# Decays of two chunks moved in the queues of a gated-delta projection

## The chip, the cores and the metric

The kernel runs on one core of a Trainium2 chip. The core has a matrix engine (TensorE, PE in the profile, with its weight loads as PEld), a vector engine (VectorE, DVE), an activation engine (ScalarE, ACT), a general engine (GpSimd, POOL) and a sync engine (SyncE, SP) that issues most DMAs. Each engine takes its instructions strictly in the order of its own queue, and waits on semaphores that other engines raise. The metric is the device time of one execution in microseconds (us), of which the median of several runs is taken.

## The reference

Two model blocks run one after the other on 512 tokens of width 1024, in float32: a block with differential and latent attention, memory cross attention and a mixture of experts, and then a block whose first layer is a gated delta rule mixer (six heads of width 128). The change lies in this mixer. Cut to what matters:

```
proj = h @ w_in                                  # 26 column tiles of 128 here
qkv  = silu(causal_depthwise_conv(proj[..., :o1], conv_w))
g    = -exp(a_log) * softplus(a_logit + dt_bias) # log decay per token and head
gc    = cumsum(chunks(g))
decay = exp(where(tril, gc[:, None] - gc[None, :], -inf))
lower = where(strict, (kb @ k.T) * decay, 0)
sol   = triangular_solve(lower, rhs, unit_diagonal=True)
intra = (q @ k.T) * decay
# a scan over the chunks then carries the state and gives the outputs
mem_o = memory_attention(mem_q, mem_k, mem_v)    # 4 heads, next to the mixer
```

The kernel uses four chunks of 128 tokens in place of the reference's shorter ones; the result of the recurrence is the same.

## The kernel before

The program is one long list of stages. Each stage adds instructions to the queues of the engines that it uses, so the order in which stages are listed is the order in every queue; nothing is reordered later. Ordering by hand is the whole schedule.

A projection is a `Linear`. Its weights come in column tiles. For each tile ScalarE rounds the raw weights to a high part (line 236), VectorE makes the low part (line 242), both two tiles ahead of use, and TensorE runs 24 matmuls (lines 299 to 301: eight input slices, three products each) into one of two PSUM banks. VectorE then takes the tile out of its bank (line 2536 in the mixer). A tile may start when its low weights are ready and when the bank of the tile two before it was taken out.

The mixer's projection is the `Linear` called gdnin, with 26 tiles numbered from 0. Tiles 0 and 1 are memory queries, 2 to 7 keys, 8 to 13 values, 14 to 19 queries, 20 to 25 gates. From tile 2 to 19 each tile is also convolved over time by VectorE (`convolve`, lines 2544 and 2546) and passed through SiLU by ScalarE (line 2526, one tile later). Other work of the mixer and of the memory attention is hung on the tiles by hand. `at_tile(j, ...)` puts stages behind tile j: on TensorE after its 24 matmuls, on ScalarE and VectorE after its weight split and its taking out, ahead of the convolution. `in_tile(j, ...)` puts them in the middle: on TensorE between the tile's two halves of 12 matmuls, on ScalarE and VectorE ahead of all of the tile's own work.

The stages that matter here:

- `decay(c, banks, free)` makes the decay matrices of chunk c for six heads, three in each of two banks, ps_out and ps_shared (q = 0 and 1). TensorE: 12 instructions in the trace (six products, line 2651). VectorE: six instructions that subtract the column sums and add a mask (line 2669). ScalarE: two exponentials of three heads (line 2696). TensorE waits for what `free` names, so that a bank isn't overwritten before it was read. Chunks 0 and 1 use the same two banks.
- The memory attention of four heads: `scored(n)` (scores on TensorE, line 892; maximum on VectorE, lines 1003 and 1004; exponentials on ScalarE, line 957), `weighed(n)` (division by the sum on VectorE, line 1032), `turned_over(n)` (transposes on TensorE, line 904; copies on ScalarE, line 973), `summed(n)` (values on TensorE, line 923).
- `key_norm(h)` and `query_norm(h)`: transposes (line 2714) and squared sums on ScalarE (line 2723), in the same two banks.
- `products(0)` behind tile 12, `turned_root(0)` behind tile 13 (copies, line 2823), and then the levels l = 1 to 5 of the triangular inverse of chunk 0, one a tile from tile 14 on: `step_u` in the tile (TensorE line 2659, ScalarE copies line 2840) and `step_r` behind it (TensorE line 2659, VectorE update line 2861). GpSimd masks a matrix for each level (line 2806).

Before the mixer's chunks GpSimd also rescales the residual in eight pairs of instructions (lines 2343 and 2344), beside the first tiles. ScalarE holds one table of functions at a time: SiLU and the exponential lie in different ones, and the trace shows a table load ahead of each switch.

Of the kernel before, what the change touches and what calls it, by code (L numbers as in the profile page):

```python
# [115 lines left out]
class Events:  # L116
# [24 lines left out]
    def need(self, eng, name, label):  # L141
        self.wait(eng, name, self.plan[name, label])
# [7 lines left out]
def program(nc, a, plan):  # L150

    with ExitStack() as ctx:
        ev = Events(nc, ctx, plan)
        done, need, step = ev.done, ev.need, ev.step
# [37 lines left out]
        ps_o, ps_m = (ctx.enter_context(nc.psum_tensor(n, [P, 512], F32)) for n in ("ps_out", "ps_shared"))  # L192
# [1430 lines left out]
        def cross_root_tile(act):  # L1623
# [5 lines left out]
                          vector=lambda dve: need(dve, "norm_act", ("cross", "R")))  # L1629
# [1015 lines left out]
        state_banks = (ps_o, ps_m)  # L2645
# [26 lines left out]
        def decay(c, banks, free):  # L2672

            def tensor(pe):
                need(pe, "gate_dve", "incl")
                for q in range(2):
                    need(pe, *free(q))
                    three(pe, banks[q], q, lambda h: col_of(GATE, c, h).to_broadcast([P, P]), lambda h: INCT, ("e", c, q))

            def vector(dve):  # L2680
                for q in range(2):
                    need(dve, "c_pe", ("e", c, q))
                    if c == 2:
                        need(dve, "conv_act", FIRST_Z - 1)
                    elif c == 3:
                        need(dve, "c_pe", ("tr", 0, q))
                    need(dve, "gate_dve", "gc")
                    three_scaled(dve, q, lambda h: DEC[c][:, h, :], lambda n, h: pair(banks[q])[:, n, :],
                                 lambda h: col_of(GC, c, h), lambda n, h: const("prev"), ALU.subtract, ALU.add,
                                 ("e", c, q))  # L2690

            def scalar(act):
                for q in range(2):
                    need(act, "c_dve", ("e", c, q))
                    h0, h1 = halves[q]
                    done(act.activation(DEC[c][:, h0:h1, :], DEC[c][:, h0:h1, :], ACT.Exp), "c_act", ("e", c, q))
            return On(tensor=tensor, vector=vector, scalar=scalar)
# [5 lines left out]
        def key_norm(h, bank, free):  # L2703
            return square_norm("k", h, lambda c: kT(h, c), FIRST_K + h, SSK, bank, free)

        def query_norm(h, bank, free):
            return square_norm("q", h, lambda c: qT(h, c), FIRST_Q + h, EQ, bank, free)
# [100 lines left out]
        def turned_root(c):  # L2808
            banks = chain_banks[c]

            def tensor(pe):
                for q in range(2):
                    need(pe, "c_dve", ("R", c, 0, q))
                    last = three_blocks(pe, banks[q], q, 0, RC[c], None)
                    done(last, "c_pe", ("T", c, q))

            def scalar(act):
                for q in range(2):
                    h0, h1 = halves[q]
                    need(act, "c_pe", ("T", c, q))  # L2820
                    if c == 0:
                        need(act, *att_mem0.last)
                    done(act.copy(TC[c][:, h0:h1, :], pair_c(banks[q], 0)), "c_act", ("T", c, q))
            return On(tensor=tensor, scalar=scalar)
# [328 lines left out]
        def at_tile(j, *stages):  # L3153
            beside[j] += stages
            chunk_steps.extend(stages)

        def in_tile(j, *stages):
            middle[j] += stages
            chunk_steps.extend(stages)

        gate_read = lambda q: ("gate_dve", "ngam")
        mem0_out = lambda o: ("att_act", ("out", att_mem0.o0 + o))
        key_squared = lambda h: ("norm_act", ("k", "square", h))
        query_squared = lambda h: ("norm_act", ("q", "square", h))
# [3 lines left out]
        at_tile(2, att_mem0.scored(0))  # L3168
        in_tile(3, On(tensor=sums_tensor, scalar=sums_scalar, vector=sums_vector))
        at_tile(3, att_mem0.weighed(0))  # L3170
        in_tile(4, decay(0, state_banks, gate_read))
        at_tile(4, decay(1, state_banks, lambda q: ("c_dve", ("e", 0, q))), att_mem0.turned_over(0), att_mem0.scored(1))
        at_tile(5, key_norm(0, ps_m, ("c_dve", ("e", 1, 1))),
                On(tensor=lambda pe: need(pe, "c_dve", ("e", 1, 0))), att_mem0.summed(0), att_mem0.weighed(1))
        at_tile(6, key_norm(1, ps_m, key_squared(0)), att_mem0.turned_over(1), att_mem0.scored(2))
        at_tile(7, key_norm(2, ps_m, key_squared(1)), att_mem0.summed(1), att_mem0.weighed(2))
        at_tile(8, key_norm(3, ps_m, key_squared(2)), att_mem0.turned_over(2), att_mem0.scored(3))
# [3 lines left out]
        at_tile(11, att_mem0.summed(3), On(scalar=key_roots_scalar, vector=key_roots_vector))  # L3181
        last_turn = ("turn_act", turns["n"] - 1)
        at_tile(12, products(0, lambda q: last_turn))
        at_tile(13, turned_root(0))
        for l in range(1, JOIN):
            in_tile(13 + l, step_u(0, l))
            at_tile(13 + l, *([query_norm(0, ps_o, key_squared(5))] if l == 4 else []),
                    *([On(tensor=lambda pe: need(pe, *mem0_out(1))), query_norm(1, ps_m, query_squared(0))] if l == 5 else []),
                    step_r(0, l))
        in_tile(19, join_u(0))  # L3190
        at_tile(19, query_norm(2, ps_o, query_squared(1)), join_r(0))
# [627 lines left out]
```

How the kernel before makes its waits and increments, by code:

```python
    def wait(self, eng, name, value):  # L135
        if self.waited.get((id(eng), name), 0) < value:
            eng.wait_ge(self.sem(name), value)
            self.waited[id(eng), name] = value
# [79 lines left out]
        def wait_evac(eng, t):  # L219
            eng.wait_ge(evacuated[t % BANKS], t // BANKS + 1)
# [7 lines left out]
        def wait_products(eng, name):  # L228
            eng.wait_ge(tile_done, BASE[name] + STAGE_OF[name][1])
# [1 line left out]
        def split_high(act, t):  # L231
            _, _, kt, m, _ = TILE[t]
            act.wait_ge(w_loaded[t % RING], 16 * (t // RING + 1))
            if t >= SPLIT:
                act.wait_ge(tile_done, t - SPLIT + 1)
            act.activation(WH[:, t % SPLIT, 0:kt * m], WRAW[:, t % RING, 0:kt * m],
                           ACT.Copy).then_inc(high_ready, 1)
# [1 line left out]
        def split_low(dve, t):  # L239
            _, _, kt, m, _ = TILE[t]
            dve.wait_ge(high_ready, t + 1)
            dve.tensor_tensor(WL[:, t % SPLIT, 0:kt * m], WRAW[:, t % RING, 0:kt * m],
                              WH[:, t % SPLIT, 0:kt * m].bitcast(F32), ALU.subtract).then_inc(low_ready, 1)
# [37 lines left out]
            def tensor_steps(self, pe, j, n0, n1):  # L281
                t = self.base + j
                if n0 == 0:
                    while scores_read:
                        need(pe, *scores_read.pop())
                    pe.wait_ge(low_ready, t + 1)
                    if t >= BANKS:
                        wait_evac(pe, t - BANKS)
                out = ps_lin[t % BANKS][0:self.m, 0:self.n]
```

## Time and profile before

| what | us |
|---|---|
| runs before | 2014.61, 2012.51, 2014.4 |
| median of them | 2014.4 |
| the profiled execution | 2007.3 |
| its span, first to last instruction | 2005.3 |
| TensorE busy in the span | 1875.6 (94%) |
| VectorE busy | 1048.4 (52%) |
| ScalarE busy | 752.5 (38%) |
| GpSimd busy | 113.0 (6%) |

The profiled execution is one more run of the same program, 0.35% under the median of the others. 2.0 us of it lie outside the span. TensorE is busy nearly everywhere, so what a change is worth is read at the places where TensorE stands still. Times of rows are microseconds from the start of the span. Consecutive instructions of one kind are merged in one row, with their count.

### The profile page before, as it was taken

To read this page: it belongs to the slowest core of one execution; us is meant where nothing else is said; L and a number is where in the kernel's file an instruction comes from. 1 tells how busy PE (TensorE), PEld (TensorE's weight loads), DVE (VectorE), ACT (ScalarE), POOL (GpSimd) and SP (SyncE) were. 2 spreads that over 40 slices of the span, in tenths; PEclk is the share of its full clock that TensorE was granted. 3 is DMA by queue.
4 is the path that set the end of the run, shared out by engine and by line. 5 is a ranking of instruction groups with operands and counts; after the bars stand their busy time and mean duration, and the time that the engine had idled before them with its cause. 6 is when DMAs were issued, how large, how long until landed. Compare 5 with 4: busy or idle time off the path is not lost.

```text
span 2005.3 us, 27517 instructions
## 1 busy us (share of the span) xinstructions
PE 1875.6 (94%) x10978; PEld 1440.2 (72%) x10978; DVE 1048.4 (52%) x2002; ACT 752.5 (38%) x1593; POOL 113.0 (6%) x104
## 2 busy tenths in 40 slices
PE   7999889999996968999879999999999999999997
PEld 5665569685553556778778888888876688888886
DVE  6767666452121158775665444634567654444444
ACT  4445855531111155533443322322356542222222
POOL 0000000001221114011200000000000000000000
PEclk9999989999998989999999999999999999999999
DMA  5100314459999941222002333232321133333321
GB/s 190 47 10 16 105 35 137 147 185 399 410 410 404 404 157 56 64 64 64 13 7 89 95 101 94 86 105 93 96 73 43 43 98 100 98 93 96 98 92 42
DMA packets 72622, 248.60 MB, mean 124 GB/s; under 512 B 9218, under 2 KB 11522, under 8 KB 71600
## 3 DMA queue, kind: packets, MB, share of 16 engines
q1 hardware_dynamic: 67088, 235.65, 33.8%
q0 software_dynamic: 5408, 11.19, 1.6%
q8 instruction: 88, 1.44, 0.3%
q14 instruction: 38, 0.31, 0.1%
HBM read 242.62 MB, written 12.59 MB: 127 GB/s over the span
## 4 chain that ended last, share of the span: by engine, by line
PE 73%; DVE 7%; DMA 4%; ACT 4%; issue 1%; SPq 0%; DVEq 0%; POOLq 0%; POOL 0%; ACTq 0%
PE ps_pair L299 18%; PE ps_pair L300 18%; PE ps_pair L301 18%; PE ps_pair L2059 5%; DMA w_places<-w_experts 2%; PE ps_turn L2659 2%; PE ps_pair L892 1%; PE ps_out L2070 1%; PE ps_shared L2070 1%; DMA split_acts_as_f<-w_experts 1%; PE ps_out L923 1%; PE ps_pair L2651 1%; PE ps_turn L904 1%; DMA g<-rows_h,g_as_int 1%; DVE scratch L2546 1%
## 5 line engine op out<-in xcount | busy, mean ns | idle before, releaser
L299 PE MATMUL ps_pair<-split_acts,w_high 128*128 128x512 f32 (+1 forms) x1816 | 720.3, 397 | 17.4 <-DVE split_acts L626 10.9
L301 PE MATMUL ps_pair<-split_acts,w_low 128*128 128x512 f32 (+1 forms) x1816 | 704.1, 388 | 0.0
L300 PE MATMUL ps_pair<-split_acts,w_high 128*128 128x512 f32 (+1 forms) x1768 | 685.0, 387 | 0.0
L299 PEld LDWEIGHTS ps_pair<-split_acts,w_high 128*128 128x128 f32 x1816 | 342.2, 188 | 100.2 <-issue 26.5
L242 DVE TENSOR_TENSOR w_low<-w_raw,w_high 128x1024 fp32r<-128x1024 f32 (+4 forms) x249 | 281.7, 1132 | 246.3 <-ACT w_high L236 244.3
L301 PEld LDWEIGHTS ps_pair<-split_acts,w_low 128*128 128x128 f32 x1816 | 342.0, 188 | 71.6
L300 PEld LDWEIGHTS ps_pair<-split_acts,w_high 128*128 128x128 f32 x1768 | 333.9, 189 | 66.2 <-issue 1.9
L236 ACT ACTIVATE w_high<-w_raw 128x1024 fp32r<-128x1024 f32 (+4 forms) x249 | 242.6, 975 | 150.1 <-PE ps_pair L301 147.7
L372 DVE TENSOR_TENSOR x<-x,ps_pair 128x512 f32<-128x512 f32 x80 | 54.9, 686 | 137.2 <-PE ps_pair L301 137.2
L2279 DVE TENSOR_TENSOR g<-g,ps_pair 64x256 f32<-64x256 f32 x31 | 13.2, 424 | 175.0 <-ACT g L2225 175.0
L3260 ACT ACTIVATE split_acts<-h 128x512 fp32r<-128x512 f32 x44 | 27.9, 633 | 200.1 <-DVE h L3273 200.1
L3255 ACT ACTIVATE h<-h 128x512 f32<-128x512 f32 x44 | 27.8, 632 | 138.4 <-DVE h L3266 138.3
L3270 DVE TENSOR_TENSOR h<-ps_pair,h 128x512 f32<-128x512 f32 x44 | 30.4, 692 | 78.5 <-PE ps_pair L301 78.5
L957 ACT ACTIVATE g<-ps_pair,columns 128x256 f32<-128x256 f32 (+3 forms) x112 | 57.4, 524 | 36.5 <-DVE columns L1011 34.4
L620 ACT ACTIVATE split_acts<-x,vectors 128x512 fp32r<-128x512 f32 x48 | 33.9, 722 | 92.5 <-DVE x L372 89.2
L2059 PE MATMUL ps_pair<-split_acts_as_f 128*64 128x256 f32 x232 | 58.6, 405 | 6.7 <-DMA w_places<-w_experts 3.1
L3266 DVE TENSOR_TENSOR h<-ps_pair,h 128x512 f32<-128x512 f32 x44 | 30.4, 692 | 58.5 <-PE ps_pair L301 52.8
L2061 PE MATMUL ps_pair<-split_acts_as_f 128*64 128x256 f32 x232 | 58.7, 405 | 0.0
L2225 ACT ACTIVATE g<-ps_pair 64x256 f32<-64x256 f32 x31 | 11.6, 375 | 124.0 <-PE ps_pair L2061 124.0
L973 ACT COPY split_acts_as_f<-ps_turn 128x512 f32<-128x512 f32 (+3 forms) x72 | 32.1, 471 | 52.9 <-PE ps_turn L904 48.5
L1011 DVE CUSTOM_DVE_ANT_0 ps_pair<-split_acts_as_f,ps_pair 128x128 f32<-128x128 f32 (+3 forms) x96 | 45.4, 508 | 10.0 <-PE ps_pair L892 9.6
L2059 PEld LDWEIGHTS ps_pair<-split_acts_as_f 128*64 128x64 f32 x232 | 32.6, 146 | 23.5 <-issue 10.5
(565 smaller groups left out, 2381.4 us busy)
## 6 DMA issues: line engine op xcount, KB each, us to landing
w_raw<-w_gu SPq DMA_DIRECT2D x88, 512.0 KB, 3.5
split_acts_as_f<-w_experts SPq DMA_DIRECT2D x42, 1024.0 KB, 19.8
w_places<-w_experts SPq DMA_DIRECT2D x35, 1024.0 KB, 18.8
w_raw<-w_down SPq DMA_DIRECT2D x32, 448.0 KB, 3.2
w_raw<-w_gdnin SPq DMA_DIRECT2D x26, 512.0 KB, 3.5
w_raw<-w_out SPq DMA_DIRECT2D x24, 512.0 KB, 3.6
x<-w_experts SPq DMA_DIRECT2D x12, 1024.0 KB, 20.2
w_raw<-w_down SPq DMA_DIRECT2D x16, 512.0 KB, 3.5
```

The lines of the kernel that those rows point to most:

```text
L236: act.activation(WH[:, t % SPLIT, 0:kt * m], WRAW[:, t % RING, 0:kt * m], ACT.Copy).then_inc(high_ready, 1)
L242: dve.tensor_tensor(WL[:, t % SPLIT, 0:kt * m], WRAW[:, t % RING, 0:kt * m], WH[:, t % SPLIT, 0:kt * m].bitcast(F32), ALU.subtract).then_i ...
L299: pe.matmul(out, wh[:, k, :], self.high(k), start=(n == 0), stop=False)
L300: pe.matmul(out, wh[:, k, :], self.low(k), start=False, stop=False)
L301: last = pe.matmul(out, wl[:, k, :], self.high(k), start=False, stop=(n == self.kt - 1))
L372: dve.tensor_tensor(X[:, j, :], X[:, j, :], out, ALU.add).then_inc(evacuated[t % BANKS], 1)
L957: done(act.activation(self.member(self.prob(n), j, w), self.member(self.bank(m), j, w), ACT.Exp, bias=COL[:, c + j:c + j + 1], scale=self. ...
L1011: done(dve.tensor_tensor_reduce(out=part, in0=mask, in1=part, scale=-scale, scalar=3e38, op0=ALU.add, op1=ALU.min, accum_out=top[:, j:j + ...
L2059: pe.matmul(out[rows, 0:256], xs, w[:, at_:at_ + 256], start=(k == 0), stop=(k == KT - 1), skip_group_check=True)
L2061: last = pe.matmul(out[high_rows, 0:256], xs, w[:, at_ + 256:at_ + 512], start=(k == 0), stop=(k == KT - 1), skip_group_check=True)
L2070: last = pe.matmul(out[n * SLOTS:(n + 1) * SLOTS, :], h[:, k * SLOTS:(k + 1) * SLOTS], w[:, k * 1024 + n * 512:k * 1024 + n * 512 + 512], ...
L2659: last = pe.matmul(pair_c(bank, part)[rows, n, :], lhs[rows, h, :], moved, start=True, stop=True)
```

## The change

The stages of chunk 0's decays are pulled apart. Their TensorE part stays in the middle of tile 4 (the fifth). Their VectorE and ScalarE parts, which stood ahead of tile 4's own work on those engines, now stand behind it. The decays of chunk 1, which stood behind tile 4 on all three engines, now stand behind tile 13 (the fourteenth), after `turned_root(0)`. The waits that guard the two banks follow: the first key norm waits for chunk 0's decays instead of chunk 1's, and the first two query norms (behind tiles 17 and 18) for chunk 1's.

```
-        in_tile(4, decay(0, state_banks, gate_read))
-        at_tile(4, decay(1, state_banks, lambda q: ("c_dve", ("e", 0, q))), att_mem0.turned_over(0), att_mem0.scored(1))
-        at_tile(5, key_norm(0, ps_m, ("c_dve", ("e", 1, 1))),
-                On(tensor=lambda pe: need(pe, "c_dve", ("e", 1, 0))), att_mem0.summed(0), att_mem0.weighed(1))
+        first_decay = decay(0, state_banks, gate_read)
+        in_tile(4, On(tensor=first_decay.tensor))
+        at_tile(4, On(vector=first_decay.vector, scalar=first_decay.scalar), att_mem0.turned_over(0), att_mem0.scored(1))
+        at_tile(5, key_norm(0, ps_m, ("c_dve", ("e", 0, 1))),
+                On(tensor=lambda pe: need(pe, "c_dve", ("e", 0, 0))), att_mem0.summed(0), att_mem0.weighed(1))
...
-        at_tile(13, turned_root(0))
+        at_tile(13, turned_root(0), decay(1, state_banks, lambda q: mem0_out(1) if q else key_squared(5)))
...
-            at_tile(13 + l, *([query_norm(0, ps_o, key_squared(5))] if l == 4 else []),
-                    *([On(tensor=lambda pe: need(pe, *mem0_out(1))), query_norm(1, ps_m, query_squared(0))] if l == 5 else []),
+            at_tile(13 + l, *([query_norm(0, ps_o, ("c_dve", ("e", 1, 0)))] if l == 4 else []),
+                    *([On(tensor=lambda pe: need(pe, "c_dve", ("e", 1, 1))), query_norm(1, ps_m, query_squared(0))] if l == 5 else []),
```

TensorE's queue behind tile 4, as a piece of the difference (- before, + after). The first two rows are the tile's last matmuls, L2651 the decays of chunk 1, L904 the transposes of the memory attention:

```order
 L300 MATMUL ps_pair0<-split_acts_50,w_high_53 128x512
 L301 MATMUL ps_pair0<-split_acts_50,w_low_54 128x512
-L2651 MATMUL ps_out<-g_60 128x128 x3
-L2651 MATMUL ps_shared<-g_60 128x128 x3
 L904 MATMUL ps_turn0<-consts_63,split_acts_as_f32_51 128x128 x4
 L904 MATMUL ps_turn1<-consts_63,split_acts_as_f32_51 128x128 x4
```

The two groups of L2651 are gone from here, so the transposes follow the tile. On ScalarE at tiles 4 and 13, where L2696 is the exponential of the decays, L236 the high part of the weights, L2526 SiLU, and L2840 the copies that level 1 needs (first fence tile 4, second fence tiles 13 and 14):

```order
 L2526 ACT_TABLE_LOAD
 L2526 ACTIVATE g_60<-scratch_58 128x512
-L2696 ACT_TABLE_LOAD
-L2696 ACTIVATE h_56<-h_56 128x384 x2
-L236 ACTIVATE w_high_53<-w_raw_52 128x1024
-L2526 ACT_TABLE_LOAD
+L236 ACTIVATE w_high_53<-w_raw_52 128x1024
 L2526 ACTIVATE g_60<-scratch_58 128x512
 L2696 ACT_TABLE_LOAD
```

```order
 L2823 COPY split_acts_as_f32_51<-ps_turn1 128x192
-L2840 COPY split_acts_as_f32_51<-ps_turn0 128x192
-L2840 COPY split_acts_as_f32_51<-ps_turn1 128x192
-L236 ACTIVATE w_high_53<-w_raw_52 128x1024
+L2696 ACT_TABLE_LOAD
+L2696 ACTIVATE h_56<-h_56 128x384 x2
+L2840 COPY split_acts_as_f32_51<-ps_turn0 128x192
+L2840 COPY split_acts_as_f32_51<-ps_turn1 128x192
+L236 ACTIVATE w_high_53<-w_raw_52 128x1024
+L2526 ACT_TABLE_LOAD
 L2526 ACTIVATE g_60<-scratch_58 128x512
```

One pair of exponentials with its table load, and one table load for SiLU, moved from tile 4 to tiles 13 and 14. On VectorE the decays of chunk 0 (L2669) now stand behind tile 4's weight split and taking out:

```order
 L2544 TENSOR_SCALAR scratch_58<-h_56,vectors_64 128x512
 L2546 SCALAR_TENSOR_TENSOR scratch_58<-h_56,vectors_64,scratch_58 128x512 x3
-L2669 SCALAR_TENSOR_TENSOR h_56<-ps_out,g_60,consts_63 128x128 x3
-L2669 SCALAR_TENSOR_TENSOR h_56<-ps_shared,g_60,consts_63 128x128 x3
 L242 TENSOR_TENSOR w_low_54<-w_raw_52,w_high_53 128x1024
 L2536 TENSOR_TENSOR h_56<-ps_pair0,h_56 128x512
```

A group of the same six, chunk 1's, stands in the changed kernel behind the taking out of tile 13 and ahead of that tile's convolution.

## Rows read from the trace of the kernel before

**Rows 1.** The page: the span.

```profile
span 2005.3 us, 27517 instructions
```

**Rows 2.** Timeline, TensorE behind tile 4: start, us, engine, line, tiles, count, [idle before]

```profile
776.79 1.65 PE L2651 MATMUL ps_out<-g 128*128 128x128 f32 x6 [6.36 <-DVE h L2669]
...
779.51 1.71 PE L904 MATMUL ps_turn<-consts,split_acts_as_f 128*128 128x128 f32 x8
...
783.07 0.50 PE L299 MATMUL ps_pair<-split_acts,w_high 128*128 128x512 f32 x1
```

**Rows 3.** Stretches: span, busy of PE, PEld, DVE, ACT, POOL, then granted clock

```profile
776.00:780.00 4.00, 3.21 (x15) 3.21 (x16) 2.47 (x7) 2.96 (x4) 0.17 (x1) 0.50 0.00 0
856.00:860.00 4.00, 2.35 (x31) 2.04 (x32) 3.89 (x5) 2.66 (x6) 1.24 (x1) 1.00 0.25 53
868.00:876.00 8.00, 8.00 (x96) 6.36 (x96) 5.68 (x8) 1.83 (x5) 1.19 (x2) 1.00 0.24 68
```

**Rows 4.** Timeline, VectorE at tiles 4 to 6.

```profile
769.02 2.51 DVE L1032 TENSOR_SCALAR split_acts_as_f<-split_acts_as_f,columns 128x256 f32<-128x256 f32 x4
...
772.32 3.52 DVE L2546 SCALAR_TENSOR_TENSOR scratch<-h,vectors,scratch 128x512 f32<-128x512 f32 x3
...
775.87 0.87 DVE L2669 SCALAR_TENSOR_TENSOR h<-ps_out,g,consts 128x128 f32<-128x128 f32 x3
776.65 0.86 DVE L2669 SCALAR_TENSOR_TENSOR h<-ps_shared,g,consts 128x128 f32<-128x128 f32 x3
...
785.17 2.33 DVE L2546 SCALAR_TENSOR_TENSOR scratch<-h,vectors,scratch 128x512 f32<-128x512 f32 x3
787.63 1.23 DVE L242 TENSOR_TENSOR w_low<-w_raw,w_high 128x1024 fp32r<-128x1024 f32 x1
```

**Rows 5.** Timeline, TensorE from tile 5 to the start of tile 7.

```profile
788.67 0.60 PE L2714 MATMUL ps_shared<-consts,g 128*128 128x128 f32 x4
789.20 1.93 PE L923 MATMUL ps_out<-split_acts_as_f,g 128*64 128x512 f32 x4
...
797.07 1.04 PE L904 MATMUL ps_turn<-consts,split_acts_as_f 128*128 128x128 f32 x8
798.03 1.99 PE L892 MATMUL ps_pair<-g,split_acts_as_f 64*128 64x256 f32 x8
799.95 0.50 PE L299 MATMUL ps_pair<-split_acts,w_high 128*128 128x512 f32 x1
```

**Rows 6.** Timeline, ScalarE at tile 4.

```profile
776.77 0.52 ACT L2696 ACTIVATE h<-h 128x384 f32<-128x384 f32 x1 [7.17 <-DVE h L2669]
...
779.03 1.28 ACT L2526 ACT_TABLE_LOAD   x1
...
780.32 0.63 ACT L2526 ACTIVATE g<-scratch 128x512 f32<-128x512 f32 x1
...
783.11 1.05 ACT L973 COPY split_acts_as_f<-ps_turn 128x512 f32<-128x512 f32 x2
```

**Rows 7.** Timeline, TensorE at level 1 of the inverse, tile 14.

```profile
857.65 0.91 PE L2659 MATMUL ps_turn<-split_acts_as_f 64*64 64x64 f32 x24 [2.11 <-ACT split_acts_as_f L2823]
...
861.47 1.61 PE L2659 MATMUL ps_turn<-split_acts_as_f 64*64 64x64 f32 x48
```

**Rows 8.** Timeline, VectorE at tiles 12 and 13.

```profile
852.23 4.41 DVE L2546 SCALAR_TENSOR_TENSOR scratch<-h,vectors,scratch 128x512 f32<-128x512 f32 x3
...
857.82 0.68 DVE L2536 TENSOR_TENSOR h<-ps_pair,h 128x512 f32<-128x512 f32 x1
```

**Rows 9.** Timeline, ScalarE at tiles 13 and 14.

```profile
857.21 0.52 ACT L2823 COPY split_acts_as_f<-ps_turn 128x192 f32<-128x192 f32 x2
858.26 0.67 ACT L2840 COPY split_acts_as_f<-ps_turn 128x192 f32<-128x192 f32 x2 [0.53 <-PE ps_turn L2659]
```

**Rows 10.** Timeline, GpSimd: its last rescaling, and a mask at tile 14.

```profile
774.29 1.88 POOL L2344 TENSOR_SCALAR x<-x,vectors 128x512 f32<-128x512 f32 x1
...
858.65 1.24 POOL L2806 TENSOR_TENSOR split_acts_as_f<-split_acts_as_f,g 128x384 f32<-128x384 f32 x1 [3.35 <-PE ps_turn L2659]
```

## The prediction

> **What bounds the kernel now.** I read the page first: TensorE is busy 94% of a span of 2005.3 us [rows 1], so an edit pays only where it shortens a stretch in which TensorE waits or works at a low clock. Then the waits of the mixer's projection, by time, and then the timeline of each engine around the two places that the diff touches. The waits name one long stall there: behind tile 4, TensorE stands still for 6.36 us in front of chunk 1's decays, until VectorE has read chunk 0's out of the same banks [rows 2]. Why VectorE is late is in its own rows: it divides the probabilities (2.51 us, to 771.53), then convolves tile 3 (its last three steps end at 772.32 + 3.52 = 775.84), and only then comes to the decays, at 775.87 [rows 4]. TensorE had finished tile 4 at 776.79 - 6.36 = 770.43. The reader is also to see the clock: in the 4 us after the stall it is granted 0.50, the lower of its two levels (1.2 of 2.4 GHz) [rows 3]. The memory attention behind it pays for that too: its transposes take from 779.51 on 1.71 us, and 1.04 at the full clock [rows 2, 5].
>
> The second place is tile 14. TensorE waits 2.11 us there for the copies of the turned root [rows 7], which ScalarE reaches at 857.21 [rows 9], behind a SiLU that waited for a convolution of 4.41 us [rows 8]. The same three steps take 2.33 us elsewhere [rows 4].
>
> **The change, part by part.**
>
> 1. *Chunk 1's TensorE part leaves tile 4.* The stretch from the end of tile 4 to the first matmul of tile 5 was 783.07 - 770.43 = 12.64 us [rows 2]. What remains in it is: a wait for the divided probabilities, which are ready at 771.53, say 771.6 with the signal (1.2 us); the transposes, 798.03 - 797.07 = 0.96; the scores, some 1.95 (799.95 - 798.03 = 1.92, taken with the rounding of the rows) [rows 4, 5]. That is 4.1 us, and tile 5 starts at 774.5 or 774.6. Its own bank and low weights are no wait: the tile before it was queued on the same two conditions, and VectorE had met both for tile 5 before it began the division at 769.02. **Gain 8.5 us.** It holds the stall, 12 instructions at the low clock (776.79 to 779.51, 2.7 us) and some 0.7 us of slow transposes. A wait of 1.2 us should not cost the clock: the one of 2.11 us at tile 14 left it at 1.00 [rows 3, 7].
>
> 2. *VectorE and ScalarE at tile 4.* From 775.84 VectorE now does the weight split (1.23), the taking out (0.68) and then the six decay steps (0.87 + 0.86) [rows 4, 8]: 777.1, 777.8, 779.5. Nothing waits for the split or for the bank earlier than tile 6. The key norm behind tile 5 waits for the decays: TensorE comes to it at 774.6 + 5.6 (one tile, 788.67 - 783.07) = 780.2, after them. ScalarE rounds the next weights at once instead of standing 7.17 us before the exponentials [rows 6]. It does SiLU at 775.9 (0.63), loads a table (1.28) and ends the second exponential near 779.5 + 0.5 = 780.0; the copies for the attention (1.05) end at 781.0 [rows 6]. TensorE wants them at 780.2 + 0.53 (789.20 - 788.67) = 780.7 [rows 5]. **Loss 0.3 us**, at least 0, and at most about 3 if ScalarE and VectorE run as late here as their slowest rows. The next meeting, transposes behind tile 6, comes at 788.9, and the probabilities should be ready by about 787: two splits, decays, a maximum and a convolution in a row. From tile 7 on VectorE waits for TensorE again, as before, so that a lead once won is kept.
>
> 3. *Chunk 1's TensorE part at tile 13.* Its 12 instructions need some 1.5 us at the full clock: 12 of them took 2.72 at half of it [rows 2, 3], which bounds it between 1.4 and 2.7. The 2.11 us stall of tile 14 lies behind them and ends with a copy that doesn't move, so they are hidden [rows 7]. If that cover were gone they would cost 1.5. Bounds 0 and 1.5 us; **cost 0**.
>
> 4. *Chunk 1's VectorE and ScalarE parts at tile 13.* VectorE: six steps after the taking out, 857.82 + 0.68 = 858.5 to 860.2 [rows 8]. ScalarE: behind the copies that end near 857.7 a table load to 859.0, exponentials to about 859.9 and 860.7, and then the copies of level 1, 860.7 to 861.4 (0.67) [rows 6, 9]. Those stood at 858.26. TensorE wants the first of them at 861.47 [rows 7]. Queued behind on ScalarE are a weight rounding, a table load (1.28) and SiLU; behind on VectorE the convolution of tile 13, a split, a taking out and the level's update, all 1.3 to 1.7 us later than before. The update ended about 1.1 us ahead of the next level's products, so that TensorE waits a few tenths there. **Cost 0.3 us**, bounds 0 and 2. In the next tile VectorE catches up: it is busy 5.68 of 8 us there [rows 3]. The number of table loads stays the same, two leave tile 4 and two come at tiles 13 and 14.
>
> On the table load the rows say that the SiLU behind one starts at 780.32, when the load from 779.03 has just ended (1.28) [rows 6]. The Trainium skill (ScalarE: Activation LUTs, What ACT_TABLE_LOAD costs) speaks against this change: it gives about 1283 ns for the load and about 1380 ns more to drain, 2.66 us for a switch. By the rows item 4 stands as it is. By the page the exponentials at tile 13 would end some 0.7 us later, the copies at 862.1, and TensorE would lose an estimated 0.6 us more. No row here has that drain, so the sum goes by the rows.
>
> 5. *Query norms.* They wait for chunk 1's decays, four tiles (some 33 us) after these are done. Cost 0. The exponentials of chunk 1 are next used after the projection. No DMA is moved, and GpSimd's queue is as before.
>
> **Sum.** 8.5 - 0.3 - 0 - 0.3 = 7.9 us. Against the profiled execution, 2007.3, that is 1999.4. The median of the runs, 2014.4, lies 7.1 us above the profiled execution, which nothing in the trace explains; a saving in a stall should be the same in both, so that the median becomes 2014.4 - 7.9 = **2006.5 us**. From the bounds the gain is 8.5 at most, with half a microsecond for the rounding, and 8.5 - 3 - 0 - 0.5 = 5 in the worse half. Medians of three runs that lie 2.1 us apart add some 1.5 either way.
>
> **The rivals.**
>
> *Lateness is handed on, still faster (chance 0.12).* VectorE does no less work between 770 and 790. If the probabilities of the second head or the copies behind tile 5 come 3 to 4 us later than worked out, TensorE waits at tiles 5 to 7 instead, and the gain is 4 to 5.5: about 2009.6. For it: VectorE's steps were slow up to 776 (3.52 against 2.33 [rows 4]). Against it: GpSimd's rescaling, the likely cause, ends at 774.29 + 1.88 = 776.2 [rows 10].
>
> *The stall moves with the decays, no difference (0.12).* Exponentials that wait for VectorE now stand ahead of the copies of level 1. If ScalarE waited 7.17 us for them again [rows 6], the exponentials would end at 859.0 + 7.2 + 0.9 = 867.1, the copies at 867.8, TensorE would stand 6.4 us from 861.47, and pay the low clock afterwards as before, 1.4 + 0.7 us. Gain 8.2 - 8.5 = -0.3: 2014.7. The same time would come if the change didn't act, because TensorE's wait at 770.43 were in truth for the probabilities. Against both: VectorE has only a split and a taking out ahead of these decays (1.9 us), no convolution, and the probabilities were there at 771.53 [rows 4, 8].
>
> *The chain of levels runs late, slower (0.04).* Levels 1 to 5 are a strict loop of products, copy, products, update over TensorE, ScalarE and VectorE. If VectorE can't absorb the 1.7 us that are put in at tile 13, every level ends late by what a tile's VectorE work exceeds the tile's time. VectorE is busy 5.68 in 8 us, 5.9 in a tile of 8.3 [rows 3]. It decides from the point where its steps are slower by 8.3 / 5.9 = 1.4 throughout. The slowest convolution is slower by 4.41 / 2.33 = 1.9 [rows 4, 8]; with all steps like it a tile's work is 11.2 us, each level ends 2.9 late, five levels give back 14.5, and the kernel ends at 2014.4 + 14.5 - 8.2 = 2020.7. Speaking for it: GpSimd's masks lie beside VectorE's work there (1.24 us [rows 10]). The Trainium skill (SBUF — State Buffer, SBUF: two separate sides) has VectorE and GpSimd share an exclusive port, which a GpSimd instruction holds for its whole length. By that rule a tile loses at most GpSimd's own time, 1.19 of 8 us [rows 3], the load stays near 7.1, and this rival falls.
>
> **How the numbers follow.** Forecast 0.72, handed on 0.12, no difference 0.12, slower 0.04. A measurement of this kernel tells some 0.2%, 4 us, from no change. Faster by more than that: the forecast and nearly all of the first rival, 0.83. Within it: 0.13. Slower by more: 0.04. The range runs from 2014.4 - 8.9 - 1.5 - 1 = 2003 (the last for what no row shows) to 2011, which takes in the handed-on case; about 0.17 lies outside.
>
> **What would show it.** In the profile after: no L2651 between tile 4 and the transposes, a wait of 1 to 1.5 us there at a clock of 1.00, tile 5 starting some 8.5 us earlier, L923 behind tile 5 waiting under 0.5 us, L2651 between the turned root and tile 14, the 2.11 us wait shrunk to about 0.6, and the level 1 products of `step_r` waiting a few tenths at most. It would be wrong if a wait of over 2 us appeared on L923 or L904 in tiles 5 to 7, if `step_r` or `step_u` in tiles 14 and 15 waited over 1 us, or if the clock still fell near 775. The steps before tile 4 and after tile 19 should take the same time as before.

## The result

| | median, us | lowest to highest | runs |
|---|---|---|---|
| before | 2013.45 | 2011.22 to 2014.61 | 4 |
| changed | 1999.8 | 1998.73 to 2001.09 | 4 |

The ratio is 0.9942, with a 95% interval of 0.9924 to 0.9959: 11.7 us faster, between 8 and 15. The changed kernel was timed against the kernel before on two more chips: 0.9960 (0.9948 to 0.9972) and 0.9941 (0.9928 to 0.9955). All runs together, 76 of before and 16 of the changed kernel, have means of 2011.8 and 2001.3 us: 10.5 us, give or take 1.2.

The forecast was 7.9 us faster, 2006.5, with a range of 2003 to 2011. The sign, the mechanism and its places were right; the time lies 3.2 us below the range. The largest part of the miss that the record can name is the base, a median of three runs. A smaller part is a gain that was too small in the sum, and 1.6 us stay open.

**The profile after.** The page:

```profile
span 1998.6 us, 27516 instructions
```

Timeline of TensorE at tiles 4 and 5, the same columns as before:

```profile
766.69 0.93 PE L2651 MATMUL ps_out<-g 128*128 128x128 f32 x6 [0.97 <-DVE g L2599]
767.46 0.83 PE L2651 MATMUL ps_shared<-g 128*128 128x128 f32 x6
772.21 1.09 PE L904 MATMUL ps_turn<-consts,split_acts_as_f 128*128 128x128 f32 x8 [1.15 <-DVE split_acts_as_f L1032]
773.23 1.99 PE L892 MATMUL ps_pair<-g,split_acts_as_f 64*128 64x256 f32 x8
...
775.15 0.50 PE L299 MATMUL ps_pair<-split_acts,w_high 128*128 128x512 f32 x1
...
780.75 0.60 PE L2714 MATMUL ps_shared<-consts,g 128*128 128x128 f32 x4
781.44 1.93 PE L923 MATMUL ps_out<-split_acts_as_f,g 128*64 128x512 f32 x4
```

The stall of 6.36 us [rows 2] is gone. In its place TensorE waits 1.15 us for the probabilities (1.2 foreseen). Tile 4 ended at 772.21 - 1.15 = 771.06 and tile 5 starts at 775.15, which is 4.09 us for the 12.64 of before: 8.55 us less, where 8.5 was foreseen. L923 starts 781.44 - 780.75 = 0.69 us after the key norm, 0.16 more than the 0.53 of [rows 5].

Timelines of VectorE and ScalarE there:

```profile
772.94 3.52 DVE L2546 SCALAR_TENSOR_TENSOR scratch<-h,vectors,scratch 128x512 f32<-128x512 f32 x3
776.50 1.23 DVE L242 TENSOR_TENSOR w_low<-w_raw,w_high 128x1024 fp32r<-128x1024 f32 x1
777.64 0.68 DVE L2536 TENSOR_TENSOR h<-ps_pair,h 128x512 f32<-128x512 f32 x1
778.24 0.86 DVE L2669 SCALAR_TENSOR_TENSOR h<-ps_out,g,consts 128x128 f32<-128x128 f32 x3
779.01 0.86 DVE L2669 SCALAR_TENSOR_TENSOR h<-ps_shared,g,consts 128x128 f32<-128x128 f32 x3
```

```profile
777.15 1.28 ACT L2696 ACT_TABLE_LOAD   x1
779.13 0.53 ACT L2696 ACTIVATE h<-h 128x384 f32<-128x384 f32 x1 [0.70 <-DVE h L2669]
779.90 0.53 ACT L2696 ACTIVATE h<-h 128x384 f32<-128x384 f32 x1 [0.25 <-DVE h L2669]
780.34 1.05 ACT L973 COPY split_acts_as_f<-ps_turn 128x512 f32<-128x512 f32 x2
```

VectorE is as late as before (3.52 us for the convolution, [rows 4]), but only ScalarE waits for its decays now. In stretches of 4 us the granted clock, the number behind GpSimd's column, is 1.00 throughout, where before it fell to 0.50 [rows 3]:

```profile
770.00:774.00 4.00, 2.85 (x17) 2.09 (x16) 3.93 (x6) 0.00 (x0) 3.90 (x4) 1.00 0.36 123
774.00:778.00 4.00, 4.00 (x18) 3.09 (x17) 3.93 (x4) 1.49 (x2) 2.70 (x2) 1.00 0.00 0
```

At tiles 13 and 14, TensorE, then ScalarE:

```profile
844.81 0.93 PE L2651 MATMUL ps_out<-g 128*128 128x128 f32 x6
845.59 0.83 PE L2651 MATMUL ps_shared<-g 128*128 128x128 f32 x6
849.94 0.92 PE L2659 MATMUL ps_turn<-split_acts_as_f 64*64 64x64 f32 x24 [0.77 <-ACT split_acts_as_f L2823]
853.76 1.61 PE L2659 MATMUL ps_turn<-split_acts_as_f 64*64 64x64 f32 x48
858.25 0.92 PE L2659 MATMUL ps_turn<-split_acts_as_f 64*64 64x64 f32 x24
866.54 0.91 PE L2659 MATMUL ps_turn<-split_acts_as_f 64*64 64x64 f32 x24
```

```profile
850.04 1.28 ACT L2696 ACT_TABLE_LOAD   x1
851.60 0.53 ACT L2696 ACTIVATE h<-h 128x384 f32<-128x384 f32 x1 [0.28 <-DVE h L2669]
852.37 0.53 ACT L2696 ACTIVATE h<-h 128x384 f32<-128x384 f32 x1 [0.25 <-DVE h L2669]
852.81 0.52 ACT L2840 COPY split_acts_as_f<-ps_turn 128x192 f32<-128x192 f32 x2
...
854.30 1.28 ACT L2526 ACT_TABLE_LOAD   x1
855.60 0.64 ACT L2526 ACTIVATE g<-scratch 128x512 f32<-128x512 f32 x1
```

VectorE and GpSimd beside them:

```profile
850.71 0.86 DVE L2669 SCALAR_TENSOR_TENSOR h<-ps_out,g,consts 128x128 f32<-128x128 f32 x3
...
852.77 2.33 DVE L2546 SCALAR_TENSOR_TENSOR scratch<-h,vectors,scratch 128x512 f32<-128x512 f32 x3
...
856.88 1.01 DVE L2861 TENSOR_TENSOR split_acts_as_f<-split_acts_as_f,ps_turn 128x384 f32<-128x384 f32 x2
```

```profile
850.94 1.02 POOL L2806 TENSOR_TENSOR split_acts_as_f<-split_acts_as_f,g 128x384 f32<-128x384 f32 x1 [3.35 <-PE ps_turn L2659]
```

Chunk 1's products fill part of the wait of tile 14, 2.11 us before [rows 7] and 0.77 now. The copies of level 1 end at 853.33, and the products that need them start at 853.76 without a wait.

One ruler serves for all that follows: **the stretch** from the first product of chunk 0's decays to level 3 of the inverse, in tile 16 (the last row of TensorE's fence above, 866.54). The same rows of the kernel before:

```profile
766.08 0.94 PE L2651 MATMUL ps_out<-g 128*128 128x128 f32 x6 [0.95 <-DVE g L2599]
...
865.96 0.91 PE L2659 MATMUL ps_turn<-split_acts_as_f 64*64 64x64 f32 x24
...
874.25 0.92 PE L2659 MATMUL ps_turn<-split_acts_as_f 64*64 64x64 f32 x24
```

The stretch took 866.54 - 766.69 = 99.85 us; before it took 874.25 - 766.08 = 108.17. That is 8.3 us, against a forecast of 7.9. (Later figures of the stretch are taken from unrounded starts, so that the last digit can differ by one from that of the rows.) The two spans differ by only 6.7 us, since other stages ended 1.6 us worse in this execution, and the medians by 13.65. So the open question was not where the 8.3 came from but why the runs show more.

### The profile page after: what moved, and what is told of

It is laid out like the page before. It is cut to its first block, busy times and chain, and to the rows that moved or that the text cites. A ratio compares the mean times of both kernels' runs of the same rounds, so it can differ in the third digit from the quotient of the medians.

```text
span 1998.6 us, 27516 instructions
## 1 busy us (share of the span) xinstructions
PE 1876.4 (94%) x10978; PEld 1440.6 (72%) x10978; DVE 1047.9 (52%) x2002; ACT 753.4 (38%) x1593; POOL 113.0 (6%) x104
## 4 chain that ended last, share of the span: by engine, by line
PE 73%; DVE 7%; DMA 4%; ACT 4%; issue 1%; SPq 0%; DVEq 0%; POOLq 0%; POOL 0%; ACTq 0%
PE ps_pair L299 18%; PE ps_pair L301 18%; PE ps_pair L300 18%; PE ps_pair L2059 5%; DMA w_places<-w_experts 2%; PE ps_turn L2659 2%; PE ps_pair L892 1%; PE ps_out L2070 1%; PE ps_shared L2070 1%; DMA split_acts_as_f<-w_experts 1%; PE ps_out L923 1%; PE ps_pair L2651 1%; DMA g<-rows_h,g_as_int 1%; DVE w_low L242 1%; PE ps_turn L2156 1%
## 5 line engine op out<-in xcount | busy, mean ns | idle before, releaser
L236 ACT ACTIVATE w_high<-w_raw 128x1024 fp32r<-128x1024 f32 (+4 forms) x249 | 243.0, 977 | 148.4 <-PE ps_pair L301 145.8
L2225 ACT ACTIVATE g<-ps_pair 64x256 f32<-64x256 f32 x31 | 11.7, 377 | 125.6 <-PE ps_pair L2061 125.6
L2059 PEld LDWEIGHTS ps_pair<-split_acts_as_f 128*64 128x64 f32 x232 | 33.4, 149 | 25.7 <-issue 11.7
```

Of the source, the lines that this page charges most:

```text
L236: act.activation(WH[:, t % SPLIT, 0:kt * m], WRAW[:, t % RING, 0:kt * m], ACT.Copy).then_inc(high_ready, 1)
L2059: pe.matmul(out[rows, 0:256], xs, w[:, at_:at_ + 256], start=(k == 0), stop=(k == KT - 1), skip_group_check=True)
```

## The experiments

### How far two executions of one kernel differ

The kernel before, unchanged.

> The kernel before, unchanged, to see how far its own runs and profiles lie apart. Theory S (spread): the gap that I missed, 13.6 us between the medians against 8.3 us in the stretch that the edit touches, is spread of the kernel before: its runs reach from 2007 to 2015 us, a profile of it again has the stall behind tile 4 at 6 to 7 us, and the rest of the time differs by where low clocks fall in other stages. Theory H (hidden): the profiled execution of before was a lucky one and the stall costs 11 to 14 us in an ordinary run (a longer stall, or a longer low clock after it): then a new profile of some 2013 us shows tile 5 starting 4 to 6 us later after tile 4 than the 12.6 us shown.

Measured: 2011.51 us (2006.97 to 2014.92, 12 runs), and 2011.76 for the 29 runs beside it (2006.94 to 2015.87). One kernel spreads over 9 us, and the mean of all is 2.6 us below the 2014.4 from which I had summed. The changed kernel on the same chip:

> The changed kernel again, on the same chip and in the same rounds as the kernel before. Theory S: the ratio comes out nearer to 1 than 0.9942, some 0.9955 to 0.996 (8 to 9 us). Theory H: again 0.993 to 0.995 (10 to 14 us).

Measured: 2002.32 us, ratio 0.9960 (0.9948 to 0.9972). That is theory S's number. It is no proof: on the third chip the ratio was 0.9941, theory H's number. Theory H falls by the trace: the stall in the new trace of before is 6.35 us, as in the first. But that trace shows something which neither theory had. TensorE and the stretches around tile 14, in this trace of the kernel before:

```profile
861.00:864.00 3.00, 3.00 (x9) 2.32 (x8) 2.89 (x4) 0.84 (x2) 0.49 (x1) 0.50 0.39 142
864.00:868.00 4.00, 4.00 (x59) 3.23 (x58) 3.69 (x6) 0.28 (x1) 0.00 (x0) 0.96 0.44 128
```

Behind the wait of tile 14 (2.13 us here, ended at 859.26) the clock was granted at 0.50, the lower of its two levels, for some 3.4 us. In the first trace it was 1.00 there. The stretch took 109.65 us, 1.5 more than in the first.

### Each part alone

The split alone, with chunk 1's decays left behind tile 4 (edit against the kernel before):

```
-        in_tile(4, decay(0, state_banks, gate_read))
-        at_tile(4, decay(1, ...
+        first_decay = decay(0, state_banks, gate_read)
+        in_tile(4, On(tensor=first_decay.tensor))
+        at_tile(4, On(vector=first_decay.vector, scalar=first_decay.scalar), decay(1, ...
```

> The split alone: chunk 0's VectorE and ScalarE parts behind tile 4's own work, but chunk 1's decays still behind tile 4. My reading: no gain and a loss, because TensorE still waits at the same place for a read that now comes 1.9 us later (split 1.23 and taking out 0.68): stall 8 to 8.5 us in place of 6.4, no gain of its own but one table load pair fewer, which nothing waits for; 0 to 2.5 us slower than before. Rival (the split is what pays, since the weight split and the taking out no longer stand behind late decays): 3 us or more faster.

Measured: 2013.1 us, ratio 1.0011 (1.0002 to 1.0020), and 110.57 us for the stretch, 2.4 more than the shortest of before. TensorE behind tile 4:

```profile
778.27 1.65 PE L2651 MATMUL ps_out<-g 128*128 128x128 f32 x6 [8.09 <-DVE h L2669]
```

The stall is 8.09 us, 1.7 longer. Alone the split loses what was foreseen; the rival that it is what pays falls.

The move alone, chunk 0's decays whole in the middle of tile 4 (edit against the changed kernel):

```
-        first_decay = decay(0, state_banks, gate_read)
-        in_tile(4, On(tensor=first_decay.tensor))
-        at_tile(4, On(vector=first_decay.vector, scalar=first_decay.scalar), att_mem0.turned_over(0), ...
+        in_tile(4, decay(0, state_banks, gate_read))
+        at_tile(4, att_mem0.turned_over(0), ...
```

> The move alone: chunk 1's decays behind tile 13, chunk 0's left whole in the middle of tile 4. My reading: most of the gain. Tile 5 starts at the same point as in the changed kernel; but ScalarE now does the exponentials at 776.8, weights, SiLU table, SiLU and the exponential table again before the attention's copies, which end near 783.5 to 784, where TensorE wants them at 780.7: a new wait of 2.5 to 3 us on L923 behind tile 5. Gain 5.5 to 6 us against before, 2.3 to 2.8 less than the changed kernel. Rival (the split is idle): the same time as the changed kernel within 1 us.

Measured: 2004.99 us, ratio 0.9967 (0.9957 to 0.9978); the stretch took 100.96 us. TensorE and ScalarE behind tile 5:

```profile
782.65 1.93 PE L923 MATMUL ps_out<-split_acts_as_f,g 128*64 128x512 f32 x4 [1.27 <-ACT split_acts_as_f L973]
```

```profile
779.71 1.28 ACT L2526 ACT_TABLE_LOAD   x1
781.00 0.63 ACT L2526 ACTIVATE g<-scratch 128x512 f32<-128x512 f32 x1
781.54 1.05 ACT L973 COPY split_acts_as_f<-ps_turn 128x512 f32<-128x512 f32 x2
782.61 1.28 ACT L957 ACT_TABLE_LOAD   x1
```

The move carries 7.2 of the 8.3 us. The split adds 1.1, by taking a switch to SiLU out from between the decays' exponentials and the attention's copies. By the ratio the move alone is 6.6 us faster than before. The wait is where I put it, but half as long: in the rows the copies stand ahead of the second exponential table (782.61), which I had placed in front of them.

### Whether the 12 instructions are hidden at tile 14

The changed kernel with chunk 1's decays behind tile 15 (edit against the changed kernel):

```
-        at_tile(13, turned_root(0), decay(1, state_banks, ...))
+        at_tile(13, turned_root(0))
...
-                    step_r(0, l))
+                    step_r(0, l),
+                    *([decay(1, state_banks, ...)] if l == 2 else []))
```

> The changed kernel with chunk 1's decays behind tile 15 in place of 13, where TensorE has no wait to hide them. My reading (they are hidden in the 2.11 us wait of tile 14): the wait of tile 14 is back at some 2.1 us, the 12 instructions cost 1.5 us of their own, tiles 13 to 16 take 1.3 to 1.6 us longer than in the changed kernel. If, beside it, a wait of that length sometimes lowers the clock (the new profile of before shows one low stretch right behind it, from 871 us), the medians differ by up to 3 us. Rival (they cost the same anywhere): within 0.5 us of the changed kernel, 9 to 10 us faster than before.

Measured: 2002.93 us, ratio 0.9952 (0.9938 to 0.9965), and a stretch of 102.66 us. The row of TensorE at tile 14:

```profile
848.71 1.35 PE L2659 MATMUL ps_turn<-split_acts_as_f 64*64 64x64 f32 x24 [2.11 <-ACT split_acts_as_f L2823]
```

The wait is back at 2.11 us, and the level's first products behind it take 1.35 us in place of 0.91 [rows 7]. The stretches say why:

```profile
846.00:850.00 4.00, 1.89 (x28) 1.38 (x26) 3.90 (x5) 1.38 (x4) 0.36 (x1) 0.87 0.07 6
850.00:854.00 4.00, 4.00 (x13) 2.99 (x12) 3.86 (x5) 1.91 (x3) 1.01 (x1) 0.70 0.34 125
```

The same kernel again, beside the changed one:

> Chunk 1's decays behind tile 15 again. The wait of tile 14 is 2.1 us. Theory D: a low stretch right behind it in this trace with a chance of some 3 in 5, and 2.3 to 2.8 us slower than the changed kernel by the medians: 1.5 us for the 12 instructions without cover, and some 1 us of low clock. If low clocks play no part: 1.3 to 1.6 us slower.

> The changed kernel a third time, as the yardstick for the three beside it on this chip, and for one more trace. Theory D (a wait of 2.1 us at tile 14 lowers the clock in some executions, a wait of 0.77 us in none): no low stretch between 845 and 880 us. Theory R (the low stretches there come at random): one in two traces has it. Against before some 9 to 10 us.

Measured: 2002.04 us (0.9951, 0.9939 to 0.9963) for the decays behind tile 15, 2001.57 us (0.9941, 0.9928 to 0.9955) for the changed kernel. The medians are 0.5 us apart where 2.3 to 2.8 were expected; with six runs each over 6 to 7 us this difference is inside the spread, and I draw nothing from it. The traces are sharper. The changed kernel has no low stretch between 845 and 880 us in its third trace either. In the kernel with the decays behind tile 15 no low clock followed the wait of 2.11 us this time (a chance of 3 in 5 had been given to one), and the stretch took 101.16 us. That is 1.4 above the 99.76 to 99.84 of the three traces of the changed kernel: the price of the 12 instructions without their cover. With a low clock behind the wait it is 102.66, another 1.5.

### Why VectorE is late at tile 4

The kernel before, with GpSimd's rescaling held back until tile 6 is done:

```
             need(pool, "roots_act", "final1")
+            pool.wait_ge(tile_done, BASE["gdnin"] + 7)
             for k in range(KT):
```

> The kernel before, with one edit: GpSimd's eight pairs of rescaling (from 748 to 776 us, beside tiles 1 to 4) wait until tile 6 is done. Theory G (VectorE is late at tile 4 because GpSimd slows it): L1032 back at 1.14 us, the convolution at 2.33, VectorE reaches the first decays 5 to 6 us earlier, the stall behind tile 4 falls from 6.4 to under 1.5 us and the low clock behind it goes: 5 to 8 us faster than before. Theory W (VectorE has too much work there whatever GpSimd does): the stall stays at 4 us or more, gain under 2.5 us. The rescaling may slow VectorE at tiles 7 to 11 instead; it has 2 to 5 us of waiting per pair of tiles there.

Measured: 2003.09 us, ratio 0.9957 (0.9941 to 0.9973). VectorE and TensorE (the added line makes every later line number one higher):

```profile
762.64 1.14 DVE L1032 TENSOR_SCALAR split_acts_as_f<-split_acts_as_f,columns 128x256 f32<-128x256 f32 x4
764.21 2.33 DVE L2547 SCALAR_TENSOR_TENSOR scratch<-h,vectors,scratch 128x512 f32<-128x512 f32 x3
```

```profile
767.50 0.93 PE L2652 MATMUL ps_out<-g 128*128 128x128 f32 x6 [0.20 <-DVE h L2670]
```

Theory G holds. With GpSimd silent the division takes 1.14 us for 2.51 and the convolution 2.33 for 3.52 [rows 4], and the stall is 0.20 us for 6.36. So the stall that the change removes was made by GpSimd's work beside VectorE, and one added wait on GpSimd brings 8.6 us (by the ratio; 5 to 8 were expected) without touching the decays. The slowing moved with the rescaling: it now runs from 785.78 to 813.09, and three convolutions beside it take 3.56, 3.54 and 3.47 us. But TensorE waits for none of this; from tile 5 on its first wait is that of tile 14.

The same line in the changed kernel:

> The same edit in the changed kernel. Theory G: the waits left near tile 4 (0.97 us in the middle of it, 1.15 us for the probabilities, some 0.2 us on L923) go, 2 to 2.5 us faster than the changed kernel, 11 to 12.5 us faster than before. Theory W: no more than 0.5 us faster than the changed kernel.

Measured: 1999.61 us, ratio 0.9934 (0.9920 to 0.9948). In the trace no wait of TensorE near tile 4 is left: the stretch took 98.11 us, 1.7 less, and the 0.97 us ahead of it went too. Against the kernel before the ratio gives 13.3 us, where 11 to 12.5 were expected; the changed kernel was not timed beside it. The two edits mostly share one saving: alone they bring 8.6 and about 10.5 us.

### Taking the wait of tile 14 away

The kernel before, with ScalarE's copies of the turned root ahead of its work for tile 13:

```
-        at_tile(13, turned_root(0))
+        root = turned_root(0)
+        in_tile(13, On(scalar=root.scalar))
+        at_tile(13, On(tensor=root.tensor))
```

> The kernel before, with one edit: ScalarE's copies of the turned root stand ahead of its work for tile 13, so that they no longer queue behind a SiLU that waits for VectorE's slowed convolution. The stall behind tile 4 stays. The wait of 2.11 us at tile 14 goes to under 0.2. Theory D: 2.1 us and the low stretches behind it, 2.8 to 3.5 us faster than before, and no low stretch between 855 and 885. Without the clock: 1.9 to 2.1 us.

Measured: 2009.45 us, ratio 0.9985 (0.9974 to 0.9996), 3 us faster. The wait is gone and no low stretch follows. A smaller wait has come one level on:

```profile
869.79 0.94 PE L2659 MATMUL ps_turn<-split_acts_as_f 64*64 64x64 f32 x24 [0.72 <-DVE split_acts_as_f L2861]
```

So 1.4 of the 2.1 us are kept. This trace also holds the longest low stretch of all, at the stall of tile 4:

```profile
774.00:790.00 16.00, 12.07 (x37) 9.76 (x38) 11.44 (x23) 9.31 (x19) 3.21 (x3) 0.50 0.09 33
```

The lower level was granted for some 17 us, where it was some 7 us in the first trace ([rows 3] is a part of it). The stretch took 110.90 us, although the wait of tile 14 is gone.

All three edits together:

> The changed kernel with the late rescaling and with the early copies of the root. The late rescaling took the waits near tile 4 away (2.3 us in its trace), the early copies should take the 0.76 us left at tile 14: 3.0 us faster than the changed kernel on the same chip, 12 to 13 us faster than before. Rival (VectorE, loaded by the rescaling at tiles 7 to 11, or ScalarE, held by the copies, is late elsewhere): no more than 1.5 us.

Measured: 1998.65 us (1994.36 to 2001.62), ratio 0.9926 (0.9913 to 0.9938), beside 0.9941 for the changed kernel on the same chip. It is ahead by 2.9 us in the medians, and the intervals overlap. In the traces the stretch is 97.58 us, 2.2 less, with the 0.97 us ahead of it gone as well. Against before the ratio gives 14.9 us, where 12 to 13 were expected. It is the fastest version measured; that it beats the changed kernel rests on the traces more than on the runs. Only 0.19 us of wait is left around tile 14:

```profile
853.38 1.61 PE L2660 MATMUL ps_turn<-split_acts_as_f 64*64 64x64 f32 x48 [0.19 <-ACT split_acts_as_f L2841]
```

### How often the low clocks come

Four more traces of the kernel before.

> Trace 3 of the kernel before, one of four for a count. Theory D: the low clock behind the stall of tile 4 is 6.8 us in some and 10 to 17 us in others (each 3.4 us more costs about 1 to 1.7 us), and a stretch of 3.4 us stands behind the wait of tile 14 in about half of them (1.6 us each); the mean time from the end of tile 4 to tile 17 over the traces is 9.5 to 11 us above the changed kernel's. Rival: 6.8 us and none in all four, the stretch costs 8.3 us in each, and the rest of the gap lies in other stages.

> Trace 4 of the kernel before, with the same two readings as the first of these four.

> Trace 5 of the kernel before, with the same two readings as the first of these four.

> Trace 6 of the kernel before, with the same two readings as the first of these four.

The stretch in all traces of the two kernels (the end is the start of level 3 in tile 16):

| trace | stretch, us | stall, tile 4 | wait, tile 14 | low clock behind tile 14 |
|---|---|---|---|---|
| before, first | 108.17 | 6.36 | 2.11 | no |
| before, second | 109.65 | 6.35 | 2.13 | yes |
| before, third | 108.36 | 6.35 | 2.12 | no |
| before, fourth | 108.30 | 6.37 | 2.11 | no |
| before, fifth | 108.35 | 6.36 | 2.12 | no |
| before, sixth | 109.68 | 6.35 | 2.12 | yes |
| changed, first | 99.84 | none | 0.77 | no |
| changed, second | 99.76 | none | 0.76 | no |
| changed, third | 99.79 | none | 0.76 | no |

The clock in the sixth of these, behind its wait that ended at 861.27:

```profile
863.00:866.00 3.00, 3.00 (x9) 2.35 (x8) 2.90 (x4) 0.83 (x2) 0.51 (x1) 0.50 0.40 146
```

The low stretch at the stall of tile 4 has the short length, 6.8 us, in all six; 17 us came in one trace and 10 us in another, the split alone with its stall of 8.09 us. So neither the 10 to 17 us that I expected in some of the last four traces nor their 9.5 to 11 us over the changed kernel came: their mean is 108.67, 8.9 more.

Over all 17 traces, those of the edited kernels among them, a wait of 2.1 us at tile 14 was followed by a low stretch in 4 of 10 traces (six of before, the split alone, two with the decays behind tile 15, the late rescaling in the kernel before), a wait of 0.8 us or less in 0 of 7. If these stretches fell at random, such a split would come about once in eleven times, so tile 14 alone doesn't settle it. Other places of the same traces say more. No low stretch in them began without a wait of TensorE, of 1.0 us or more, shortly before its start or around it. Two waits far from this edit were followed by one in some executions and not in others, as that of tile 14: a wait of 1.45 to 1.65 us near 403 us (line 1742) in 8 of 16 traces, and a wait of 1.0 us near 440 us (line 1779) in 3 of 17. The latter in the sixth trace of before, with its clock (no other wait stands between them):

```profile
441.29 0.49 PE L1779 MATMUL ps_shared<-g,consts 128*128 128x128 f32 x2 [1.01 <-DVE g L1841]
```

```profile
443.00:446.00 3.00, 3.00 (x10) 2.46 (x10) 2.37 (x12) 0.72 (x2) 0.00 (x0) 0.52 0.90 310
```

So waits down to 1.0 us have gone ahead of a low clock; what decides in which executions it comes isn't shown. The mean of the stretch is 108.75 us before and 99.80 after, so the edit is worth **8.95 us** there.

## Why the prediction was partly wrong

**Part 1, chunk 1's products leave tile 4 (8.5 us).** Right: 8.55 measured, with a wait of 1.15 us for the 1.2 foreseen. The transposes take 1.09 us (1.04 at the full clock [rows 5], 1.71 before). The stall, the low clock and the slow transposes are gone.

**Part 2, VectorE and ScalarE at tile 4 (loss 0.3).** Right in kind, 0.16 measured. The split is what keeps it small: without it the wait is 1.27 us.

**Part 3, the products hidden at tile 14 (0).** Right: uncovered they cost 1.4 us, by the trace without a low clock.

**Part 4, ScalarE and VectorE at tiles 13 and 14 (loss 0.3).** Too much. No wait followed. Level 2's products stand 858.25 - 853.76 = 4.49 us behind those of level 1, as in the kernel before (865.96 - 861.47), so the cost was 0. The rows show what I had overlooked. GpSimd's mask at tile 14 now runs beside the decay steps (850.94 and 850.71), which take 0.86 us as ever, and no longer beside the convolution of tile 13. That convolution takes 2.33 us, in all three traces of the changed kernel; in the kernel before, with the mask beside it (858.65 [rows 10]), it took 2.96:

```profile
859.05 2.96 DVE L2546 SCALAR_TENSOR_TENSOR scratch<-h,vectors,scratch 128x512 f32<-128x512 f32 x3
```

That gives back 0.63 us. The level's update ends at 856.88 + 1.01 = 857.89, 0.36 us ahead of the products that need it. Without the 0.63 us, by an estimate from these rows, TensorE would have waited 0.27 us, the 0.3 of the forecast.

The rule of the Trainium skill (ScalarE: Activation LUTs, What ACT_TABLE_LOAD costs) that a switch costs 2.66 us isn't borne out: the load takes 1.28, and SiLU follows at 855.60 a load that began at 854.30, as the rows of ScalarE above show. With that drain the exponentials would have begun 1.1 us later, and by an estimate from the rows the copies of level 1 would have ended near 854.2, later than the 853.76 at which their products began.

**Part 5, the query norms (0).** Right. TensorE has no wait from level 3 up to 950 us in either trace, and from level 3 to the start of the next level both take 8.28 us.

**The steps that failed.** The first and larger is in the sum: "a saving in a stall should be the same in both, so that the median becomes 2014.4 - 7.9". The saving does show in the traces, but 2014.4 was a median of three runs and 2.6 us too high: the mean over 76 runs is 2011.8. I had the hint, since the profiled execution at 2007.3 lay 7.1 us below, which I called unexplained and did not put into the range. The kernel's runs reach over 9 us, and I allowed 1.5 for this.

The second is a term that I put at nothing, in part 1, in the sentence on the clock: "the one of 2.11 us at tile 14 left it at 1.00". I took one execution for a rule, to argue that a wait of 1.2 us is harmless, and never asked what it means if a wait of 2.1 us does cost the clock at times. A low stretch followed it in 4 of 10 traces, at 1.4 to 1.5 us each, and followed none of the shorter waits that the change leaves at tile 14. That is 0.5 to 0.6 us on the average which belonged on the gain's side. The wait of 1.15 us at tile 4 was followed by no low stretch in the six traces that have it; as one of 1.0 us elsewhere was, this doesn't show that it is harmless. The sum of 7.9 should have been 8.3 + 0.6 = 8.9, as measured.

| part of the miss, 2006.5 - 1999.8 = 6.7 us | us |
|---|---|
| base: 2014.4 against the mean of 76 runs, 2011.8 | 2.6 |
| gain: 7.9 against 8.95 in the traces | 1.0 |
| the four changed runs of the result lie below the mean of all 16, 2001.3 | 1.5 |
| open: 8.95 in the traces, 10.5 in the runs | 1.6 |

The third row is the spread of the runs and nothing that the forecast could have known. With a base of 2011.8 and 8.9 us the answer would have been 2002.9.

**What stays open.** The runs give 10.5 us (about 1.2 either way), the traces 8.95. The rest, 1.6 us, is hardly more than the uncertainty. It isn't seen in the traces: outside the stretch, the six traced executions of the kernel before take 1900.1 us in the mean (1897.1 to 1902.5) and the three of the changed kernel 1899.5 (1898.0 to 1901.9). Longer low clocks at the stall of tile 4, as in one trace, would add to it, but six traces of the kernel before have none. I leave it open.

**The rivals.** None came. The stall did not move with the decays: VectorE reaches them 1.8 us after the convolution (850.71, behind one that ended at 848.93), 1.9 worked out. The handed-on lateness is real in kind, 0.16 us on L923, and grows to 1.27 when the split is left out. The chain of levels did not run late. The rule of the Trainium skill on the port that VectorE and GpSimd share (SBUF — State Buffer, SBUF: two separate sides), by which that last rival fell, would also foresee the slowing at tile 4, and the trace agrees in that VectorE's division and convolution are back at their short times once GpSimd is silent.

## What to carry to other kernels

Before placing a step behind another engine's read, look what makes the reader late; here one wait on GpSimd, which had no hurry, removed nearly the same stall as moving the step. Work that fills a wait pays twice if that wait can cost the clock, so count the waits of 1 to 2 us as well as the long ones. What is moved on one engine also moves what runs beside it: here decay steps that GpSimd doesn't slow took the place of a convolution that it does. When runs of one kernel reach over 0.4%, take a saving from the trace and the base from many runs, and ask of every clock row whether another execution would show it too.

## What was not expected of the hardware

A wait of TensorE of 2.1 us, always the same to 0.02 us, was followed by some 3.4 us at the lower clock level in 4 of 10 executions and by none in the others. It cost 1.4 to 1.5 us where it came. A wait of 1.0 us at another place was followed by one in 3 of 17 executions. At a stall of 6.35 us the clock fell every time, while TensorE still stood, for some 7 us in six traces of the kernel before and for 17 us in one trace of a kernel that does the same up to there. A VectorE convolution of three steps took 2.33 us alone and 2.96, 3.52 or 4.41 us beside GpSimd's work, while decay steps that read PSUM took 0.86 to 0.87 us each time, one group of them beside a GpSimd mask of 1.02 us.
